# A decoder step on one core: input rows loaded as column halves around the first weight piece

## What is computed

```python
def rmsnorm(x, g):
    return _rms(x) * g                     # _rms: x * rsqrt(mean(x * x) + EPS), per token

mix, ... = token_mixers(rmsnorm(h, prm['norm_mix_g']), ...)
    proj = a @ prm['w_in']                 # D_MODEL 1024 -> z 512 | xbc 1024 | dt 8 | u 512 | v 512
    z, xbc, dt_raw, u, v = jnp.split(proj, ...)
    # xbc: causal convolution over 4 tokens, silu; then the state-space recurrence
h = h + mix
h = h + moe(rmsnorm(h, ...))               # 32 experts, top 4: w_up 1024 x 2048, w_down 1024 x 1024 each
h = h + (p @ w_ple_proj) * sigmoid(rmsnorm(h, ...) @ w_ple_gate)
```

## Time and profile before

| | |
|---|---|
| median of 3 runs | 1124.59 us (1124.33 to 1125.14) |
| the profiled execution | 1124.53 us; its span from first to last instruction 1122.8 us |
| PE busy | 1083.8 us, 97% |
| DVE, ACT, POOL busy | 380.0, 162.9, 33.7 us |
| moved by DMA | 433.95 MB, 387 GB/s on average |

### The profile page before, as it was taken

The page is one execution under the profiler, slowest core; times in us unless marked ns, Lnnn a source line. Parts: engine busy times, 40 slices in busy tenths (PEclk is TensorE's granted clock), DMA queues, the critical chain, the costliest instruction groups (busy, mean ns, idle before and its releaser), DMA issues.

```text
span 1122.8 us, 16073 instructions
## 1 busy us (share of the span) xinstructions
PE 1083.8 (97%) x6446; PEld 452.2 (40%) x6446; DVE 380.0 (34%) x973; ACT 162.9 (15%) x371; POOL 33.7 (3%) x80
## 2 busy tenths in 40 slices
PE   9999999999999999999899999999999999999997
PEld 6664454333333333333333343433333324343334
DVE  3867565232222222222131323231313222222266
ACT  3544132000000000000001010100000101010023
POOL 2300130000000000000000000000000000000000
PEclk9999999999999999999999999999999999999999
DMA  9824968999999999999999999999999999999951
GB/s 330 295 105 140 381 234 352 431 430 430 432 428 435 430 431 433 431 432 430 432 434 431 431 430 431 429 430 432 433 431 434 432 430 426 434 428 423 426 231 42
DMA packets 30728, 433.95 MB, mean 387 GB/s; under 512 B 4928, under 2 KB 6224, under 8 KB 15964
## 3 DMA queue, kind: packets, MB, share of 16 engines
q1 hardware_dynamic: 29008, 428.54, 90.5%
q0 software_dynamic: 1456, 4.48, 1.2%
q10 hardware_dynamic: 220, 0.33, 0.1%
HBM read 429.03 MB, written 4.30 MB: 386 GB/s over the span
## 4 chain that ended last, share of the span: by engine, by line
PE 69%; DMA 26%; DVE 2%; ACT 2%; issue 1%; SPq 0%; DVEq 0%; ACTq 0%
PE bank L1133 27%; DMA ring<-in_w_up_dram 20%; PE bank L1189 14%; PE bank L1107 6%; PE bank L684 5%; PE bank L805 3%; DMA arena<-in_w_down_dram 3%; DMA ring<-in_w_down_dram 3%; PE bank L1086 3%; PE bank L708 1%; PE bank L1165 1%; PE bank L666 1%; DVE arena L1709 1%; PE bank L1223 1%; PE bank L997 1%; PE bank L1083 1%
## 5 line engine op out<-in xcount | busy, mean ns | idle before, releaser
L1133 PE MATMUL bank<-ring,aT 128*64 128x512 f32 x1536 | 345.1, 597 | 21.2 <-DMA ring<-in_w_up_dram 21.2
L1133 PEld LDWEIGHTS bank<-ring,aT 128*64 128x64 f32 x1536 | 109.0, 137 | 239.9 <-issue 210.4
L1189 PE MATMUL bank<-ring,arena 128*64 128x512 f32 x768 | 169.7, 594 | 3.2 <-DMA ring<-in_w_down_dram 2.5
L2135 DVE TENSOR_TENSOR h<-h,bank 128x512 f32<-128x512 f32 (+1 forms) x90 | 61.5, 683 | 178.9 <-PE bank L1107 176.8
L1133 PE MATMUL bank<-arena,aT 128*64 128x512 f32 x512 | 114.8, 595 | 0.0
L2163 DVE COPY aT<-bank 64x512 f32<-64x512 f32 x32 | 22.2, 693 | 248.6 <-PE bank L1189 248.6
L1517 ACT ACTIVATE arena<-arena 128x256 f32<-128x256 f32 x64 | 26.7, 418 | 521.3 <-DVE arena L2153 521.3
L2153 DVE TENSOR_SCALAR arena<-bank 128x256 f32<-128x256 f32 x64 | 27.2, 425 | 216.3 <-PE bank L1133 214.9
L1189 PEld LDWEIGHTS bank<-ring,arena 128*64 128x64 f32 x768 | 54.2, 137 | 103.6 <-issue 100.9
L1107 PE MATMUL bank<-aT,arena 128*32 128x512 f32 (+1 forms) x180 | 78.3, 622 | 0.0
L1133 PEld LDWEIGHTS bank<-arena,aT 128*64 128x64 f32 x512 | 35.2, 137 | 73.3 <-issue 71.7
(11 more groups left out here) (379 smaller groups left out, 765.4 us busy)
## 6 DMA issues: line engine op xcount, KB each, us to landing
ring<-in_w_up_dram SPq DMA_DIRECT2D x38, 4096.0 KB, 27.8
ring<-in_w_down_dram SPq DMA_DIRECT2D x21, 4096.0 KB, 29.0
arena<-in_w_up_dram SPq DMA_DIRECT2D x13, 4096.0 KB, 28.3
ring<-in_w_up_dram SPq DMA_DIRECT2D x19, 2048.0 KB, 29.5
arena<-in_w_down_dram SPq DMA_DIRECT2D x7, 4096.0 KB, 28.8
ring<-in_w_down_dram SPq DMA_DIRECT2D x6, 2048.0 KB, 12.2
arena<-in_w_up_dram SPq DMA_DIRECT2D x6, 2048.0 KB, 31.4
ring<-in_w_in_dram SPq DMA_DIRECT2D x3, 2048.0 KB, 14.3
```

The source lines that it names most:

```text
L1133: mm = pe.matmul(bank[n][CAP * hf:CAP * hf + CAP, :], xT[:, odd, 2 * j + a, :], up_cols(x, j, a, hf, n), start=False, stop=(j == 3 and a = ...
L1189: mm = pe.matmul(bank[4][CAP * hf:CAP * hf + CAP, :], actT[:, b, t, :], tile_of(x, UP_TILES + t)[:, 1024 * b + 512 * hf:1024 * b + 512 * h ...
L2135: tt(part, part, bank[5 + j % 2][at:at + ROWS[c], :], ALU.add).then_inc(s_free[j % 2], 1)
```

## The change

The x rows are loaded in column halves: columns 0 to 511 of all three chunks, then weight piece 0, then columns 512 to 1023 (one semaphore, `xb_in`, for all three), then the other pieces. TensorE transposes the first halves only, then multiplies k = 0 of four tiles, then transposes the second halves, and goes on with k = 1 and k = 2, 3. Five fillers stand ahead of the first transpose in place of eight; the fillers between the transposes (eight in all) go, and two stand behind the first halves. VectorE copies the halves in the new order. ScalarE first runs a Square over one column, then the squares, which wait for both halves, and only then issues the ten parameter loads. The rest is as it was.

```diff
-    jobs += [(("xT", *ch), 1, None) for ch in both]
+    jobs += [(("xT", c, hf), 1, None) for hf in range(2) for c in range(NCH)]
...
@@ SP @@
-            sp.dma_start(h[:, 0, :], xr[:, 0, :]).then_inc(x_in[0], 16)
-            sp.dma_start(h[:, 1, :], xr[:, 1, :]).then_inc(x_in[1], 16)
-            sp.dma_start(h[0:T_S, 2, :], I["x_sample"].rearrange("b s d -> (b s) d")).then_inc(x_in[2], 16)
-
+            xs_r = I["x_sample"].rearrange("b s d -> (b s) d")
             w_in = I["w_in"][0].rearrange("(k p) n -> p k n", p=P)
             o = SSD + CONV
+            for c in range(2):
+                sp.dma_start(h[:, c, 0:512], xr[:, c, 0:512]).then_inc(x_in[c], 16)
+            sp.dma_start(h[0:T_S, 2, 0:512], xs_r[:, 0:512]).then_inc(x_in[2], 16)
             for q, ks in enumerate(XBC_PIECES):
+                if q == 1:
+                    for c in range(2):
+                        sp.dma_start(h[:, c, 512:D], xr[:, c, 512:D]).then_inc(S["xb_in"], 16)
+                    sp.dma_start(h[0:T_S, 2, 512:D], xs_r[:, 512:D]).then_inc(S["xb_in"], 16)
                 sp.dma_start(w_xbc[:, ks, :], w_in[:, ks, SSD:o]).then_inc(xbc_in[q], 16)
@@ PE @@
-            keep_clock(8, 7, idle_rows)
+            keep_clock(5, 7, idle_rows)
...
             for c in range(NCH):
                 pe.wait_ge(x_in[c], 16)
-                for hf in range(2):
-                    transposed(("xT", c, hf), h, c, 4 * hf)
-                    keep_clock(4 if (c, hf) == (0, 1) else 1, 7, idle_rows)
+                transposed(("xT", c, 0), h, c)
+            keep_clock(2, 7, idle_rows)
...
             for c in range(NCH):
-                for hf in range(2):
-                    stored(pe, ("xT", c, hf))
-            project_xbc(range(4), range(0, 2))
+                stored(pe, ("xT", c, 0))
+            project_xbc(range(4), range(0, 1))
+            pe.wait_ge(S["xb_in"], 48)
+            for c in range(NCH):
+                transposed(("xT", c, 1), h, c, 4)
+            project_xbc(range(4), range(1, 2))
             project_xbc(range(4), range(2, 4))
+            for c in range(NCH):
+                stored(pe, ("xT", c, 1))
@@ ACT @@
+            act.wait_ge(S["vinit"], 1)
+            step(act.activation(junk_x[:, 0:1], ss_x[:, 0:1], ACT.Square))
+            for c in range(NCH):
+                r = slice(0, ROWS[c])
+                act.wait_ge(x_in[c], 16)
+                act.wait_ge(S["xb_in"], 48)
+                squares(junk_x[r, :], h[r, c, :], ss_x[r, c:c + 1], "sumsq", c)
+
             act.dma_start(prow[0:24, :], I["state_conv"][0].rearrange("b k n -> (b k) n")).then_inc(S["par_in"], 16)
...
-            act.wait_ge(S["vinit"], 1)
-            for c in range(NCH):
-                r = slice(0, ROWS[c])
-                act.wait_ge(x_in[c], 16)
-                squares(junk_x[r, :], h[r, c, :], ss_x[r, c:c + 1], "sumsq", c)
@@ DVE @@
-            turned("xT", 8, CH)
+            turned("xT", 8, [(c, hf) for hf in range(2) for c in range(NCH)])
```

More of the change, by code:

```diff
@@ L258, in build @@
             "bup_parts bup_stored cmask_ok consts conv_ok cv_out dec_in dt_in sel8_ok dtabs dtadd dtexp dtln "
-            "eac_ok fin_ss fss g_ok g_ready gex gf_in gl_ok g_in rdiag_ok rs_ok zuv_ok tap_ok nac_ok rsg_ok rsv_ok vz_ok last_in h0_in h0t_used hf_out hfin hss ident_ok idle_ok "
+            "eac_ok fin_ss fss g_ok g_ready gex gf_in gl_ok g_in rdiag_ok rs_ok zuv_ok tap_ok nac_ok rsg_ok rsv_ok vz_ok last_in xb_in h0_in h0t_used hf_out hfin hss ident_ok idle_ok "
             "lexp m1_ok m2_ok m3_ok m_ok mask_ok mix_done mix_ok mss h_ok ngm_ok npass_ok "
@@ L1275, in _, with squares @@
             act.dma_start(grow[0:KD, :], I["norm_mix_g"][0].rearrange("(k p) -> k p", p=P)).then_inc(S["g_in"], 16)
+            def squares(scratch, src, sums, sem, n):
+                if n:
+                    act.wait_ge(S[sem], n)
+                act.activation(scratch, src, ACT.Square, accum_out=sums).then_inc(S[sem], 1)
+            act.wait_ge(S["vinit"], 1)
[5 more added lines that the diff above has]
+                squares(junk_x[r, :], h[r, c, :], ss_x[r, c:c + 1], "sumsq", c)
             act.dma_start(prow[0:24, :], I["state_conv"][0].rearrange("b k n -> (b k) n")).then_inc(S["par_in"], 16)
```

## The result

The changed kernel takes 1127.26 us (median of 22 runs, 1125.10 to 1131.54), the kernel before 1124.97 us in the same sessions. The ratio is 1.002, with a 95% interval of 1.0013 to 1.0027: 2.3 us slower, where 1.7 us faster was forecast. Eight of its 22 runs took at most 1126.02 us, a time that runs of the kernel before reach as well: the loss is not in every execution.

A forecast was written before the change was run, and what follows sets the result against it. The expert stage was taken to run at the weight stream's pace, started by TensorE's chain in the first 21 us. Sum: 3.5 - 1.2 - 0.6 = 1.7 us earlier, 1122.9 us from 1124.53; range 1121.6 to 1125.6 us.

The forecast's parts named there:

- The stream would be ahead: Loads of x and weights: second halves at 7.3 to 8.1 us, piece 2 at 11.2 to 12.1 in place of 13.4.
- 2.3 us** earlier: End of the projection on TensorE: `rsb` at 16.1 us in place of 18.4.
- they are all there at 14.3 + 4.7 = 19.0 us: Landing of ScalarE's ten parameter loads, wanted at 18.3 us; a wait of 0.6 us was taken.
- rival 2: TensorE's start: clock stays low through k = 0, four matmuls take 4.0 us, total 1124.2 or 1125.4 us; chance 0.12.
- Rival 3: `par` bank: parameters come after 20.6 us, ScalarE's loads held while SP is held; slower, 1127.0 us; chance 0.14.
- Rival 4: Before 175 us: gain eaten by a transfer that doesn't move with TensorE; no change, 1124.5 us; chance 0.10.
- k = 0 at 6.9 us: Start of the projection on TensorE: 3.5 us earlier than 10.41 us.
- the landing of the first half: First x load: a half of 256 KB saves 0.75 us and lands at 3.4 us.
- three issues more on SP: SP's issue of loads: 3 x 0.45 us more, hidden because SP is ahead of the engines.
- the slack of w_spatial: Loads before 30 us: w_spatial and the biases have over 2 us of slack.
- the norm work ahead of `rsb`: VectorE's norm work, 3.2 us, ends at 14.1 (14.9) us, ahead of `rsb` at 16.1.
- the first paragraph: Whole kernel: if TensorE comes earlier to every trigger, the full DMA stretch from 175 us begins and ends equally earlier.

The follow-up runs named there:

- par_late_only: Kernel before with only the ten parameter loads moved behind the squares; x loads as they were; 1124.58 us, ratio 0.9989 to the kernel before.
- before_again: The kernel before, unchanged, profiled and timed again; 1125.26 us, ratio 0.9996.
- fill6: The changed kernel plus six filler matmuls ahead of TensorE's wait for the parameters; 1125.89 us, ratio 1.0001 to the kernel before.
- x_first: As best, but all six half loads of x issued ahead of weight piece 0; 1127.14 us, ratio 1.0014 to the kernel before.
- sp_holds: The changed kernel, but SP waits for the parameters before issuing w_spatial and everything behind it; 1128.07 us, ratio 1.0016 to the kernel before.
- par_mid: The changed kernel with the ten parameter loads issued behind the one-column Square, ahead of the squares; 1126.42 us, ratio 1.0003 to the kernel before.
- par_first: The changed kernel with the ten parameter loads back right behind the gain row; 1125.85 us, ratio 0.9995 to the kernel before.
- best: The edit of par_behind plus more fillers (six at the start, one behind each first half, three more) on the changed kernel; 1124.31 us, ratio 0.9989.
- par_behind: The changed kernel with parameter wait and transposes moved behind the last four blocks of projection tile 0; 1125.73 us, ratio 0.9994 to the kernel before.
- after_again: The changed kernel itself, profiled and timed once more; 1127.57 us, ratio 1.0017 to the kernel before.

## Why the prediction was wrong

**The stream would be ahead: wrong.** The prediction has the second halves at 7.3 to 8.1 us, piece 1 at 8.6 to 9.4 and piece 2 at 11.2 to 12.1 us. They landed at 9.2, 10.3 and 13.3 us. It worked with 350 GB/s for the first 5 us and took the 216 GB/s of the earlier trace rows half as the work of the parameter loads; par_late_only has the drop without them, and in the change it stands from 3 to 5 us (205 and 221 GB/s). Cutting x in halves changes the order of the same bytes, and piece 2 comes when it came. The term "**2.3 us** earlier" for `rsb` measured 0.9 us (17.35 against 18.25): k = 0 was 0.2 us late, the second halves 0.4, and k = 2 began at 13.37 us in place of 12.1, after 0.49 us of waiting for piece 2. before_again has its `rsb` another 0.6 us earlier than before (17.77 against 18.41 in the chain), since the clock rose earlier; against it the change gains 0.3 us. The path had moved from x to the weights, and there the change has nothing to give.

**"they are all there at 14.3 + 4.7 = 19.0 us": wrong, and this decided the sign.** They were there at 20.85 us. The squares wait for all second halves and began at 9.35 in place of 7.3 us, but squares and issues then took less than forecast, so the last issue ended at 15.0 us, 0.7 us late. The larger part is what 4.7 us stood for: it was the time from the last issue's end to the queue's last packet. That held (19.4 - 15.0 = 4.4 us), but the landing came 1.5 us behind the last packet. The sum gave a wait of 0.6 us from 18.3; measured are a wait of 1.20 us from 19.7 and a start 0.3 us behind before.

**What a wait of TensorE costs: missing.** The prediction weighed the clock only for the start (rival 2) and priced the wait for the parameters at its own length. The clock was at half behind it: 3.48 us for 2.14, 0.81 for 0.50, 1.7 us in all, more than five times the 0.3 us of lateness. fill6 shows it: the same wait, filled, and the loss is gone. Not every wait has this price: in the change itself the waits of 0.47 and 0.49 us for pieces 0 and 2 had matmuls at full pace behind them, and so had the 2.30 us of x_first. That the throttled clock is the default and activity releases it is what the Trainium skill, "TensorE: Matmul & The Clock Gate", Part 1, states; fill6 against the change agrees with it, and the rule alone doesn't tell which of these waits is followed by a low stretch. It stood in the prediction and was applied to the start only.

**The rivals.** Rival 3 named the place (the `par` bank), the point that decides (20.6 us) and the sign, at 0.14. Its mechanism is refuted: sp_holds has the same landing with SP silent. Rival 2 was undervalued at 0.12: in five of the seven profiles with five fillers and none between the transposes, k = 0 ran at the low clock (2.55 to 4.18 us), and in none of the seven with more fillers. Its price was overvalued, since a faster k = 0 only waits for piece 2: `rsb` began at 17.35 us in the change and at 17.62 to 17.96 us in four of the five late ones (19.75 in par_mid, where piece 0 was late too). So the low clock there cost some 0.3 to 0.6 us, a part of why par_first is no faster than before. Rival 4 is refuted: the first expert matmul lies anywhere from 168.9 to 174.0 us, and what follows takes 953.0 to 955.9 us with no relation to it.

**What was right.** k = 0 at 6.9 us (7.09), the landing of the first half, three issues more on SP at no cost that a trace shows, the slack of w_spatial, the norm work ahead of `rsb`, and the first paragraph: what happens before 175 us reaches the end, within the 3 us by which the rest varies.

**What stays open.** Where the slow stretch of the loads between 3 and 7 us comes from: it is there with and without parameter loads, in every order of x and weights. Why ten loads of 130 KB in all take 6 us from the last issue. Why the landing was 1.5 us behind the last packet. Which waits are followed by the low clock. And whether best is truly faster than before: the interval says by 0.02 to 0.2%.

## What to carry to other kernels

Before a load is moved behind other work, add up when it lands, not when its last packet moves, and put it against the moment at which its reader comes after the gain; here ten loads of 130 KB in all needed 6 us from the last issue. A wait of TensorE costs its length and can cost a stretch at the low clock behind it, here 1.7 us behind a wait of 1.20 us: put work that doesn't need the data ahead of the wait (par_behind), or fillers into it. And when the first input is made to come earlier, look at what lands next: the order of the bytes changed, their sum didn't, and the third weight piece still came at 13.3 us.

## What the runs showed of the hardware

- In every one of the fourteen profiles the stream of loads has at least one slow microsecond between 3 and 7 us (166 to 260 GB/s in the slowest, against 393 to 426 from 10 to 11 us), in each of the three orders of x and weights that were tried.
- Ten small loads on ScalarE's queue landed about 6 us after the last issue began (6.1 us in the change, 6.8 in after_again, and 5.9 in sp_holds, where SP issued nothing beside them); in the change that was 1.5 us after the queue's last packet.
- VectorE's twelve taps took 6.02 us beside GpSimd's casts and subtractions (sp_holds), and 3.49 us without (the change).
- The same kernel's expert stage took 953.0 us in one execution and 955.9 us in another. Over the fourteen profiles the longer ones are those with a granted clock of 0.57 to 0.66 from 1014 to 1022 us.
- Low clock behind a wait of TensorE: behind 1.20 us (the change) and 2.29 us (sp_holds) there was a stretch at 0.50, behind 0.49 us (the change) and 2.30 us (x_first) none.
